# Projection and attention of a hybrid decoder block as one program, with five pieces of attention inside the last pair of products

## What is computed

```python
h = rms_norm(x, norm_in)
u_a, v_a, z_a, q_b, k_b, v_b, z_b, gate_a, gate_b = split(h @ w_in)     # each 2048 x 1024
y_a = chunked_spatial_gating(gelu(u_a), rms_norm(gelu(v_a), norm_v), w_s, b_s) * silu(z_a)
y_b = stick_breaking_attention(q_b, k_b, v_b) * silu(z_b)                # 8 heads of 128
merged = sigmoid(gate_a) * (y_a @ w_o_gmlp) + sigmoid(gate_b) * (y_b @ w_o_sb)
out = rms_norm(x + merged @ w_out, norm_final)

# attention, for query t and key s < t:
#   weight[t, s] = sigmoid(z[t, s]) * product over s < j < t of (1 - sigmoid(z[t, j]))
```

## Time and profile before

| | |
|---|---|
| median of 3 runs | 2500.92 us (2499.0 to 2501.75) |
| profiled execution | 2500.69 us, of which the span of the trace is 2498.8 |
| TensorE busy | 2452.6 us, 98% |
| VectorE, ScalarE, GpSimd busy | 1567.6, 1285.3, 1227.4 us |
| projection, on TensorE | to 1452 us |
| attention, on TensorE | 1456 to 2163 us |

### The profile page before, as it was taken

How to read it: one execution, slowest core, us unless ns; L and a number is a source line. 1 busy time by engine, 2 the same in 40 slices (tenths; PEclk the granted TensorE clock), 3 DMA queues, 4 the chain that set the end, 5 groups by cost and what they waited for, 6 DMA issues and landing times. The chain is left out here.

```text
span 2498.8 us, 34385 instructions
## 1 busy us (share of the span) xinstructions
PE 2452.6 (98%) x11669; PEld 2036.1 (81%) x11669; DVE 1567.6 (63%) x2046; ACT 1285.3 (51%) x2316; POOL 1227.4 (49%) x1095
## 2 busy tenths in 40 slices
PE   7999999999999999999999989999999999999998
PEld 5888888878888888888888868888888888788887
DVE  7554455564576534555555578888788888633676
ACT  6553334433355534244444477777777777511342
POOL 2682022343334400145555557778877777724554
PEclk9999999999999999999999999999999999999999
DMA  3465544433332344455565454344343443488642
GB/s 118 152 222 200 168 139 126 131 105 122 105 97 79 99 136 151 140 155 176 175 179 177 147 163 128 99 117 139 116 117 115 111 122 122 173 288 279 226 160 110
DMA packets 282109, 367.47 MB, mean 147 GB/s; under 512 B 15832, under 2 KB 164320, under 8 KB 281952
## 3 DMA queue, kind: packets, MB, share of 16 engines
q1 hardware_dynamic: 278352, 358.94, 45.6%
q10 hardware_dynamic: 3600, 6.56, 0.7%
HBM read 243.80 MB, written 121.63 MB: 146 GB/s over the span
## 5 line engine op out<-in xcount | busy, mean ns | idle before, releaser
L1351 PE MATMUL in_bank<-carried_hi,in_w_hi 128*128 128x512 f32 x1540 | 605.3, 393 | 8.9 <-DVE carried_last L1143 3.9
L1354 PE MATMUL in_bank<-carried_hi,in_w_lo 128*128 128x512 f32 x1540 | 599.7, 389 | 0.0
L1353 PE MATMUL in_bank<-carried_lo,in_w_hi 128*128 128x512 f32 x1540 | 599.5, 389 | 0.0
L573 POOL TENSOR_TENSOR in_sums<-carried_stage 128x512 f32<-128x512 f32 x55 | 75.3, 1369 | 598.9 <-DMA carried_stage<-in_w_in 357.0
L1351 PEld LDWEIGHTS in_bank<-carried_hi,in_w_hi 128*128 128x128 f32 x1540 | 289.3, 188 | 72.6 <-DVE carried_last L1143 5.9
L1978 DVE TENSOR_TENSOR_SCAN att_rest<-att_z_ps,att_rest 128x512 f32<-128x512 f32 (+3 forms) x288 | 317.1, 1102 | 37.7 <-ACT att_z_ps L1924 21.9
L1354 PEld LDWEIGHTS in_bank<-carried_hi,in_w_lo 128*128 128x128 f32 x1540 | 289.1, 188 | 60.7
L1353 PEld LDWEIGHTS in_bank<-carried_lo,in_w_hi 128*128 128x128 f32 x1540 | 289.3, 188 | 58.0
L732 ACT ACTIVATE in_w_hi<-in_sums 128x512 fp32r<-128x512 f32 x220 | 138.3, 630 | 344.5 <-PE in_bank L1354 225.3
L1008 DVE TENSOR_TENSOR in_w_lo<-in_sums,in_w_hi 128x512 fp32r<-128x512 f32 x220 | 216.4, 984 | 44.9 <-ACT in_w_hi L732 40.9
L1878 POOL TENSOR_TENSOR carried_lo<-carried_wide,carried_hi 128x512 fp32r<-128x512 f32 x152 | 196.7, 1296 | 0.0
(11 more groups left out here) (240 smaller groups left out, 5398.7 us busy)
## 6 DMA issues: line engine op xcount, KB each, us to landing
carried_stage<-in_w_in SPq DMA_DIRECT2D x112, 512.0 KB, 4.6
carried_wide<-ya_T SPq DMA_DIRECT2D x64, 256.0 KB, 3.5
uz_T<-in_o SPq DMA_DIRECT2D x32, 256.0 KB, 5.1
carried_wide<-in_w_in SPq DMA_DIRECT2D x8, 1024.0 KB, 8.8
v_sums<-carried_wide SPq DMA_DIRECT2D x8, 1024.0 KB, 8.5
in_sums<-v_sums SPq DMA_DIRECT2D x8, 1024.0 KB, 6.2
carried_stage<-v_sums SPq DMA_DIRECT2D x8, 1024.0 KB, 6.2
va<-carried_wide SPq DMA_DIRECT2D x8, 1024.0 KB, 8.7
```

The lines of the kernel that those rows point to most:

```text
L1351: pe.matmul(bank[:, :], hi, a_hi[:, i, k], start=opens and k == 0, stop=False, skip_group_check=True)
L1353: pe.matmul(bank[:, :], hi, a_lo[:, i, k], start=False, stop=False, skip_group_check=True)
L1354: mm = pe.matmul(bank[:, :], lo, a_hi[:, i, k], start=False, stop=k == HALF_K - 1, skip_group_check=True)
```

## The change

- The scopes and blocks of the first two stages are joined. `Shared` allots memory for both: attention's tiles lie on the places of the projection's `sums`, `w_hi`, `w_lo`, `o` and `x_sb`, with tiles aligned to 4 bytes and padding between them. The eight banks of PSUM are shared by number: 0 to 2 are `z_ps`, 3 to 5 `t_ps`, 6 and 7 `y_ps` and `f_ps`. The barrier between the stages goes; its place is taken by waits for single events of the last pair, where attention first writes to a place (`ends`).
- The projection's semaphores are cleared at the end of GpSimd's attention program. To have enough of them, `a_hi_done` and `a_ready` become one counter each in place of seven, with counts in the order in which the products are made.
- Z0 to Z4 (`EARLY_Z` = 5) move into the last pair. TensorE makes logits 0 to 2 between P7 and P5, 3 between P5 and P4, 4 between P4 and P3. The roundings and rests of items 0 to 7 and the sigmoids and scans of these pieces are woven into ScalarE's and VectorE's parts of the pair. GpSimd's parts stay where they are.
- On SyncE attention's first loads, items 8 to 15, follow directly on the last pair's stores; the waits for the last stores stand behind them.

The diff without lines that are only shifted:

```diff
@@ scalar, pair(n) of the projection
+                if n == LAST - 1:
+                    for i in range(3):
+                        early_split(i)
...
                 act.activation(o11, bank_a[n % 2][:, :], func1).then_inc(c11_done, 1)
                 if n == LAST - 1:
-                    for i in range(3):
-                        early_split(i)
+                    for i in range(EARLY_Z - 2):
+                        sigmoids(i)
...
                 act.activation(o22, o22, func2).then_inc(f22_done, 1)
                 if n == LAST - 1:
-                    for i in range(3, 6):
-                        early_split(i)
+                    early_split(3)
+                    sigmoids(EARLY_Z - 2)
+                    early_split(4)
...
                 act.activation(o21, o21, func2).then_inc(f21_done, 1)
                 if n == LAST - 1:
-                    for i in range(6, w.n_early):
-                        early_split(i)
+                    early_split(5)
+                    sigmoids(EARLY_Z - 1)
+                    early_split(6)
...
                 act.activation(u2_of(n), u2_of(n), func1).then_inc(f12_done, 1)
+                if n == LAST - 1:
+                    early_split(7)
@@ vector, pair(n) of the projection
                 sum_u2(n)
+                if n == LAST - 1:
+                    for i in range(3):
+                        early_rest(i)
...
                 rest_next(P7, n)
+                if n == LAST - 1:
+                    begin_scans()
+                    for i in range(EARLY_Z - 2):
+                        scan(i)
                 sum_c22(n)
                 if n == LAST - 1:
-                    for i in range(3):
-                        early_rest(i)
+                    early_rest(3)
+                    scan(EARLY_Z - 2)
+                    early_rest(4)
...
                 sum_c21(n)
                 if n == LAST - 1:
-                    for i in range(3, 6):
-                        early_rest(i)
+                    early_rest(5)
+                    scan(EARLY_Z - 1)
+                    early_rest(6)
...
                 sum_c12(n)
                 if n == LAST - 1:
-                    for i in range(6, w.n_early):
-                        early_rest(i)
+                    early_rest(7)
@@ tensor, pair of the projection
                 product(P7, bank_b[b], g, n)
...
+                if isinstance(n, int) and n == LAST - 1:
+                    pe.wait_ge(c11_done, FREE_2 + LAST - 1)
+                    pe.wait_ge(u3_done, FREE_2 + LAST - 1)
+                    pe.wait_ge(c12_done, FREE_2 + LAST - 1)
+                    for i in range(EARLY_Z - 2):
+                        logits(i)
                 wait_bank(P5, n)
                 product(P5, bank_c[b], g, n)
+                if isinstance(n, int) and n == LAST - 1:
+                    logits(EARLY_Z - 2)
                 wait_bank(P4, n)
                 product(P4, bank_d, g, n)
+                if isinstance(n, int) and n == LAST - 1:
+                    logits(EARLY_Z - 1)
@@ sync of attention
             for i in range(w.n_early):
                 load_raw(RAWS + i)
+            for n in range(2):
+                sp.wait_ge(ends["y_stored"][n], 16 * NT // 2)
+            for n in ("stored11", "stored22", "stored21"):
+                sp.wait_ge(*ends[n])
@@ scalar of attention, sigmoids(n) and copy_weights(m)
+                if n == 0:
+                    act.wait_ge(ends["mixed"], 2 * NT)
+                    act.wait_ge(ends["biased"], 2 * NT)
+                elif n == QT:
+                    act.wait_ge(ends["w_ready"][P3], ends["last"])
+                    act.wait_ge(ends["sum_done"][3], ends["last"])
+                elif n == 8:
+                    act.wait_ge(*ends["stored21"])
...
+                elif m == W_BUFS - 1:
+                    act.wait_ge(*ends["stored11"])
+                    act.wait_ge(*ends["stored22"])
@@ tensor of attention
                 elif e == "B":
+                    if i == 0:
+                        for n in ("c11_done", "u3_done", "c12_done", "c21_done", "gained"):
+                            pe.wait_ge(*ends[n])
                     turn_weights(i)
@@ hybrid_block
-        norm_and_project(nc, x, norm_in, w_in, norm_v, w_s, b_s, w_o_gmlp, w, s, carried)
-        attention(nc, w_o_gmlp, w_o_sb, w, s, carried)
+        with ExitStack() as both:
+            shared = Shared(Scope(nc, both, "att"))
...
+            @block.scalar
+            def _(act):
+                sigmoids, run = scalar2(act)
+                scalar1(act, sigmoids)
+                run()
...
```

More of the change, by code:

```diff
@@ new lines, in norm_and_project @@
+    sc = Scope(nc, memory, "in")
+    a_hi, a_lo = (half[:, :, :].rearrange("p i (k t) -> p i k t", k=HALF_K) for half in (carried.hi, carried.lo))
+    h_T = carried.wide[:, :].rearrange("p (k t) -> p k t", k=KT)
+    w_hi, w_lo, sums, o, x_sb = shared.w_hi, shared.w_lo, shared.sums, shared.o, shared.x_sb
+    ident = carried.ident
+    gain = sc.sb("gain", [P, KT])
+    sq_sum = sc.sb("sq_sum", [P, TILES, 2])
+    mean_sq = sc.sb("mean_sq", [P, TILES])
+    inv_rms = sc.sb("inv_rms", [P, TILES])
@@ new lines, in norm_and_project @@
+    PIECES = 2 * HALF_K
+    PIECE_LOADS = {2: [0, 1], 3: [2, 3], 5: [4], 6: [5], 7: [6, 7]}
+    PIECE_SUMS = {3: [0], 4: [1], 5: [2], 6: [3], 7: [4, 5]}
+    PIECE_STORES = {4: [0], 5: [1], 6: [2]}
+    y = [x_sb[:, n] for n in range(2)]
+    mask_in = x_sb[:, 0].rearrange("p (g t) -> p g t", g=GROUPS)
+    low, high = slice(0, HALF_K), slice(HALF_K, KT)
+    first, second = slice(0, CW), slice(CW, GROUP)
+    h11, h12, h21, h22 = h_T[:, low, first], h_T[:, low, second], h_T[:, high, first], h_T[:, high, second]
@@ new lines, in norm_and_project @@
+    b11, b12 = stage[:, low, 0:P], stage[:, high, 0:P]
+    b21, b22 = stage[:, low, P:WT], stage[:, high, P:WT]
+    s1, s2, s3, s4 = (sums[:, i] for i in range(4))
+    left = {P1: b11, P6: s2, P2: b12, P7: s3, P5: s1, P4: b22, P3: s4}
+    sum_of = {P5: 0, P6: 1, P7: 2, P3: 3}
+    x_all = x_sb[:, :, :].rearrange("p a (k t) -> p (a k) t", t=CW)
+    right = [{P1: h11, P6: h11, P2: h21, P7: h12, P5: h12, P4: h21, P3: h22},
+             {P1: h11, P6: x_all, P2: h21, P7: h12, P5: h11, P4: h21, P3: h22}]
@@ new lines, in attention @@
+    y_stored, pa_stored = carried.y_stored, sc.sems("pa_stored", 2)
+    y_done, f_read, f_done = carried.y_done, sc.sem("f_read"), sc.sem("f_done")
+    by_vector = w.items[:w.n_early]
+    events, vector_events = w.events[w.n_early:], w.vector_events[w.n_early:]
+    splits = [item for item in w.items if item[0] != "v" and item not in by_vector]
+    split_of = {item: i for i, item in enumerate(splits)}
+    hi_of = {item: i for i, item in enumerate(item for item in w.items if item[0] != "v")}
@@ new lines, in gpsimd, with rest_of_split, weights @@
+    def gpsimd(pool):
+        def rest_of_split(item):
+            hi, lo = halves_of(carried, item)
+            src, _, _ = raw_of(item)
+            pool.wait_ge(split_hi, hi_of[item] + 1)
+            pool.tensor_tensor(lo, src, hi.bitcast(F32), ALU.subtract).then_inc(split_done, 1)
+        def weights(n):
+            r, left, width = w.pieces[n][3], w.left(n), w.width(n)
+            a = slot[n % SLOTS][:, 0:width]
+            if n in w.diagonals:
+                own = slot[n % SLOTS][:, width - P:width]
+                pool.wait_ge(rest_done, n + 1)
+                pool.affine_select(out=own, in_=own, compare_op=ALU.is_gt, fill=0.0, base=0, pattern=[[-1, P]],
+                                   channel_multiplier=1).then_inc(masked, 1)
+                pool.wait_ge(masked, w.diagonals.index(n) + 1)
+            pool.wait_ge(scanned, n + 1)
+            pool.tensor_tensor(a, a, rest[r][:, left + 1:left + width + 1], ALU.mult).then_inc(weighted, 1)
+        for e, i in events:
+            if e == "K":
+                rest_of_split(i)
+            elif e == "Z":
+                weights(i)
+        free_first()
@@ L2090, in _ @@
                     project_a(i)
+        return logits, run
+    return sync, gpsimd, scalar, vector, tensor
 def chunk_cols(c):
```

2998 lines of the change are left out of this document (1495 added, 1503 removed).

## The result

The changed kernel takes **2543.02 us** (median, 2541.01 to 2545.36), beside 2500.34 us for the kernel before: a ratio of 1.0168, interval 1.0156 to 1.0180. It is 43 us slower. Where one execution of a run lies far outside the rest (6374.72 us in a_wr_sp_b, 3517.86 us in b_pad256), the median given here is that of the others. The forecast was 2505.0 with a range of 2500 to 2508. The profiled execution has a span of 2541.5 us, 42.7 more than before.

A forecast was written before the change was run, and what follows sets the result against it. The prediction took TensorE, busy 98% of the span, as the bound. Late first product with v 3.6, half clock 0.6 and a small part of a slow rest's 0.9 gave 4.3: 2500.69 + 4.3 = 2505.0 us, range 2500 to 2508.

The forecast's parts named there:

- Edits with one answer: Side edits: merged counters, tiles aligned to 4 bytes with padding, waits for landed stores; each 0, padding bounded at +-0.5 us.
- Part 2: Logits 0 to 2 ahead of P5 in the last pair: new TensorE gap of 1.2 us, first logits at 1445.3.
- the end shifted otherwise than P(0): Sign of being wrong: kernel's end and attention's first product with v, P(0), don't shift alike.
- Part 1: Stage change: removes 1.7 us of barrier; clearing semaphores at the end of GpSimd's attention program costs nothing.
- Part 3: VectorE and ScalarE in the last pair wait in turn: c21 ends at 1455.1, c12 at 1459.95 (before 1452.98).
- Part 4: TensorE's first turn and SyncE's store wait for c12; loads 5.1 us later, first product with v 3.6 us later.
- Part 5: Some 8 us gap before logits 8 halves TensorE's clock until about 1473.2, adding 0.6 us at the first product with v.
- The sum: Whole kernel: 3.6 + 0.6 = 4.2, with a small part of the slow rest's 0.9: 4.3 us slower.
- loads crowded: Rival at the DMA engines behind the late store: item 9 takes 6.3 us instead of 5.0, 2506.9 us; chance 0.33.
- the change does what it says: Rival: TensorE never held by loads or c12, gaps of 8.8 us go less a new 1.2, 2493.1 us; chance 0.07.

The follow-up runs named there:

- a_wr_sp_b: Repeat of the changed kernel with tiles laid out anew and SyncE's eight loads issued between the last pair's stores; 2499.10 us.
- b_pad256: Kernel before with 256 bytes of padding ahead of w_hi, keeping places modulo 256; 2499.95 us, ratio 0.9999.
- a_wr: Changed kernel with tiles laid out anew (weights at 128 modulo 256, rests 32 bytes ahead of a multiple of 64), order of work untouched; 2502.98 us, ratio 1.0010.
- b_both: Kernel before with both the projection's weights and attention's rests moved by padding, as in the changed kernel; 2539.60 us, ratio 1.0162.
- a_wr_sp: a_wr with SyncE's first eight later attention loads issued between the last pair's stores instead of behind all four; 2498.43 us.
- m1: Block left out; matmuls and GpSimd multiplies from tiles at chosen starts; matmuls start every 0.2267 us with both weight tiles at 128, 0.2334 at 256 and 320.
- m2: Block left out; eight weight starts by four moving-operand starts, plus more GpSimd distances; matmuls start every 0.2266 to 0.2345 us.

## Why the prediction was wrong

**The step that failed** is one clause under "Edits with one answer": tiles aligned to 4 bytes with padding keep the operands' form, 0, bound +-0.5. They keep shape, type and stride, but not the distance of the operands' starts. The term was 39.6 us: 30 in the projection, 10 in attention, not in one rival and so not in the range. The rows gave no bound, as the prediction itself says ("nothing in the rows separates the two"); the error was to turn that into +-0.5 instead of asking how many instructions read the moved tiles. They are 4620 matmuls of the projection's products, with the moved tiles as weights, and 1344 of its wide ones, with the moved tiles as the moving operand: one clock more in each would already be 2.5 us, more than the whole of Part 2. A wide range would have been the honest answer. One of the prediction's own signs of being wrong did show: the end shifted otherwise than P(0), which is 31.9 us later (1500.36 against 1468.45) in a span that is 42.7 longer; the rest arises in attention.

**Part 1**, the barrier: right. No stage change stands in the trace, and nothing of it shows elsewhere: in front of the merge TensorE waits 1.1 us (1.0 before).

**Part 2**, the gap in front of logits 0: 1.2 forecast, 0.89 after, 1.04 in a_wr. Taking the shift of b_both (28.84) off, the first logits start at 1444.2 in the frame of the earlier trace rows and not at 1445.3: 0.3 from the gap, and product P7 is through 0.8 earlier than estimated from c22. That frame is good to a microsecond or two: the first logits of a_wr and a_wr_sp start at 1443.13 and 1445.48.

**Part 3**, the ladder: right to a tenth. Counted from the first logits, c21 ends at 9.89 (forecast 9.8), c12 at 14.64 (14.65).

**Part 4**, who waits for c12: right in mechanism and nearly in size. Gap before the first turn 2.25 (2.4), in front of logits 8 7.27 and 8.0 in a_wr (some 8). vb was there 3.7 us after its issue (4.1), item 9, for which ScalarE waited until 1494.63, 5.4 after its own at 1489.23 (5.0). a_wr_sp shows it: with the loads earlier, the gap falls to 2.2 and the time by 4.5. P(0) comes 27.31 behind the first logits (26.8). As these come 1.1 earlier than forecast, P(0) is 3.0 later than in b_both (1500.36 against 1497.40), not 3.6.

**Part 5**, the clock: forecast to stay at half until 1473.2, that is 3.6 us behind logits 8. It was longer. The windows of the changed kernel:

```profile
1488.00:1489.00 1.00, 1.00 (x6) 0.67 0.00 0
...
1497.00:1498.00 1.00, 0.21 (x1) 0.50 1.07 383
...
1504.00:1505.00 1.00, 1.00 (x4) 0.50 1.07 322
1505.00:1506.00 1.00, 1.00 (x7) 0.80 0.40 114
```

From logits 8 on it is 7.6 us at 1.2 GHz (0.80 in the last row puts the rise at 1505.4), and the clock had fallen before, at 1488.3, behind the shorter gap of 2.25 us in front of the first turn (the logits' matmul at 1488.82 takes 0.63 us, those ahead of that gap 0.39), which the forecast didn't have. The Trainium skill, "TensorE: Matmul & The Clock Gate", section "Why this matters for your kernels", warns of long idle gaps between bursts. The trace agrees that the clock falls behind idle time, but it fell behind the gap of 2.25 us; the long one, 7.27 us, found it at half already. Part of that stretch is still spent waiting for VectorE, so the price in the total is small: P(0) 3.0, all together 3.4. The 0.4 between them has the sign of the forecast's 0.6 for the clock, but is far below what these medians can tell, so the size of this term isn't shown.

**The sum** of these parts was 4.3. Measured it is 3.4 for the changed kernel against b_both, and 2.7 (0.2 to 4.8) for the changed kernel with a repaired layout, a_wr, against the kernel before. There the end does move with P(0): P(0) is 1.5 later (1469.98 against 1468.45) and the span 1.5 longer (2500.3 against 2498.8). The rivals: *loads crowded* had the sign right for the wrong reason, as item 9 took 5.4 us and not 6.3; *the change does what it says* (2493.1) would have needed loads that the order of SyncE's queue didn't allow. With those and three pieces, 2496.3 is within 3.2 us of it.

## What to carry to other kernels

Padding is an edit. When a diff moves tiles, list the start of each tile that an engine reads in bulk, before and after, as the distance to the other operand, and count the instructions: here distances changed by 128 and 64 bytes cost 30 us over 5964 matmuls, and 40 of 43 us came back with no change to the work. When a loss is spread evenly over a stretch in which the diff changes no order, look at means and counts per window first, not at the gaps.

When two stages are joined, the loads of the second should be moved as well: work made inside the last pair had to be paid with loads queued behind that pair's last store, and issuing them between the stores was worth 4.5 us.

## What the runs showed of the hardware

- A fp32r matmul of 128x128 weights by 128x512 starts every 0.2266 to 0.2272 us when both operands begin at the same place modulo 256, every 0.2286 to 0.2290 when the weights' place is 64 bytes below, and every 0.2323 to 0.2345 otherwise, at a granted clock of 1.00 (m1, m2; steps of 32 bytes, and one pair at a distance of 4). 0.2334 - 0.2267 = 0.0067 us, 16 clocks. Pair f of m1, one half of the weights at distance 0 and one at 192, is between, 0.2311. In the kernels the loss in starts per window is 1.8 to 2.4%, not the full 3%; the wide products lose less, with means of 390, 394 and 393 ns after and 389 before. Attention's products with v show next to nothing of it: their three matmuls start 0.234 and 0.231 us apart with the turned weights at 0 modulo 256 (before), 0.236 and 0.230 with them at 128, the place of v (a_wr; medians of 224). So the figures are shown for long runs of products as in m1, m2 and the projection only. The runs don't show why, in either case.
- GpSimd's multiply of two 128x512 float32 operands takes 1.09 us at distances of 4 or 8 bytes modulo 16, 1.27 to 1.30 at 0 or 12 (26 pairs; with the first operand off a multiple of 16 only distances of 0 and 12 were tried). The best layout is thus not the most aligned one: two tiles that both begin on a multiple of 32 are the slow case, and the kernel before was fast because its multiply reads the rests from one column (4 bytes) behind their start.
- VectorE shows nothing of the sort in these two layouts: its scans, which write the rests, take 1102 ns on the mean before and 1103 after.
